# Attention transposes of 64 queries on alternating 64-row tiles, with shared PSUM copies

## The reference, cut to what matters

```python
s_s = jnp.einsum('bcgrd,bcgkd->bcgrk', qs, k_g).astype(jnp.float32) * scale
p_s = masked_softmax(s_s, m_s)
o_s = jnp.einsum('bcgrk,bcgkd->bcgrd', p_s, v_g.astype(jnp.float32))
...
s_w = jnp.einsum('bcgrd,bkgd->bcgrk', qs, kw).astype(jnp.float32) * scale
p_w = masked_softmax(s_w, m_w)
o_w = jnp.einsum('bcgrk,bkgd->bcgrd', p_w, vw.astype(jnp.float32))
...
o = g[..., 0:1] * o_c + g[..., 1:2] * o_s + g[..., 2:3] * o_w
```

## Time and profile before

| | |
|---|---|
| median of three runs | 3684.43 us |
| the profiled execution's own time | 3682.82 us |
| its span, first to last instruction | 3681.0 us |
| PE busy, whole span | 3291.9 us (89%) |
| mean granted TensorE clock | 0.941 of full speed |
| the attention stage, first score to last product | 1963.6 to 2398.6 us |

### The profile page before, as it was taken

How to read it: one execution, slowest core, us unless ns; L and a number is a source line. 1 busy time by engine, 2 the same in 40 slices (tenths; PEclk the granted TensorE clock), 3 DMA queues, 4 the chain that set the end, 5 groups by cost and what they waited for, 6 DMA issues and landing times. The chain is left out here.

```text
span 3681.0 us, 56062 instructions
## 1 busy us (share of the span) xinstructions
PE 3291.9 (89%) x22000; PEld 2951.9 (80%) x22000; DVE 1769.3 (48%) x3212; ACT 942.5 (26%) x1458; POOL 1110.8 (30%) x799
## 2 busy tenths in 40 slices
PE   6886979999999987979667999989687999999986
PEld 5885959999999985869545666657577999999985
DVE  4566046454454446340478888810217454454443
ACT  4544033121111114021124666600114111111111
POOL 1222203333333320323013555400121333333330
PEclk9997979999999997989789999989798999999998
DMA  4213432111111125320231000057202111111112
GB/s 180 73 58 102 145 138 68 46 47 47 46 47 47 46 89 191 119 81 29 99 120 54 2 2 2 2 171 238 98 26 84 47 46 47 47 47 46 47 51 90
DMA packets 75778, 272.75 MB, mean 74 GB/s; under 512 B 9306, under 2 KB 19938, under 8 KB 73330
## 3 DMA queue, kind: packets, MB, share of 16 engines
q1 hardware_dynamic: 73810, 262.99, 20.6%
q10 hardware_dynamic: 1728, 6.34, 0.4%
HBM read 245.47 MB, written 33.10 MB: 76 GB/s over the span
## 5 line engine op out<-in xcount | busy, mean ns | idle before, releaser
L1407 POOL TENSOR_TENSOR w_hi<-w_raw,misc 128x1024 fp32r<-128x1024 f32 x197 | 381.0, 1934 | 2050.5 <-DMA w_raw<-in_w 783.6
L1409 POOL TENSOR_TENSOR w_lo<-w_raw,w_hi 128x1024 fp32r<-128x1024 f32 x197 | 495.1, 2513 | 28.4 <-issue 0.4
L1612 PE MATMUL PA<-hB_hi,w_hi 128*128 128x344 f32 x1512 | 327.9, 326 | 47.4 <-DVE hB_lo L613 23.2
L1612 PE MATMUL PB<-hB_hi,w_hi 128*128 128x344 f32 x1488 | 319.1, 323 | 19.8 <-DVE hB_lo L1796 17.1
L1612 PE MATMUL PB<-hB_lo,w_hi 128*128 128x344 f32 x1488 | 317.6, 322 | 19.5 <-POOL w_lo L1409 19.5
L1612 PE MATMUL PA<-hB_lo,w_hi 128*128 128x344 f32 x1512 | 324.6, 323 | 0.0
L1612 PE MATMUL PA<-hB_hi,w_lo 128*128 128x344 f32 x1416 | 301.9, 322 | 0.0
L385 DVE SCALAR_TENSOR_TENSOR zb<-ub,vec,zb 128x1024 f32<-128x1024 f32 x48 | 158.3, 3297 | 297.1 <-ACT zb L357 297.1
L1612 PEld LDWEIGHTS PA<-hB_hi,w_hi 128*128 128x128 f32 x1512 | 257.2, 191 | 53.2 <-issue 23.9
L1612 PE MATMUL PB<-hB_hi,w_lo 128*128 128x344 f32 x1392 | 294.7, 320 | 0.0
L1612 PEld LDWEIGHTS PB<-hB_hi,w_hi 128*128 128x128 f32 x1488 | 251.9, 189 | 22.9 <-issue 18.3
(11 more groups left out here) (438 smaller groups left out, 6275.6 us busy)
## 6 DMA issues: line engine op xcount, KB each, us to landing
w_raw<-in_w SPq DMA_DIRECT2D x197, 512.0 KB, 3.3
pages<-in_pages SPq DMA_DIRECT2D x64, 384.0 KB, 4.2
cosT<-in_mw SPq DMA_DIRECT2D x32, 512.0 KB, 3.8
sinT<-in_mw SPq DMA_DIRECT2D x32, 512.0 KB, 4.5
mt<-in_mw SPq DMA_DIRECT2D x32, 512.0 KB, 3.9
x_dram<-X SPq DMA_DIRECT2D x3, 4128.0 KB, 12.0
X<-x_dram SPq DMA_DIRECT2D x3, 4128.0 KB, 13.7
mw<-in_mw SPq DMA_DIRECT2D x4, 2048.0 KB, 22.8
```

The lines of the kernel that those rows point to most:

```text
L1407: pool.tensor_tensor(w_hi[b], w_raw[b], zero.broadcast_to([P, 1024]), ALU.add)
L1409: pool.tensor_tensor(w_lo[b], w_raw[b], w_hi[b].bitcast(F32), ALU.subtract).then_inc(sem("w_split"), 1)
L1612: mm = pe.matmul(PS[ps][:, c, 0:CH], w[:, w0:w0 + P], x[:, k, c * CH:(c + 1) * CH], start=(k == 0 and n == 0), stop=(k == K - 1 and n == 2))
```

## The change

Each 128 x 128 transpose becomes two of 64 queries: rows 0 to 63 of the `ring` tile (e = 0) go to bank PC, rows 64 to 127 (e = 1) to bank PD, one after the other, so that neighbours use the array's two 64-row tiles. A bank now holds 64 queries of both halves, not 128 of one half. All transposes of a group wait for both halves' probabilities and for all copies of the group before, and both `t*_done` come with the last pair. `pt` is two buffers of [128, 2, 512] instead of four of [128, 512]; a copy writes runs of 64 at a distance of 128. ACT copies PC in every group and PD in odd groups; DVE copies PD in even groups only. `pt_even_ready` and `pt_odd_ready` take the place of `pt1_ready`.

```diff
@@ transposes(g) on TensorE
+            pe.wait_ge(sem("p_ready"), 2 * (2 * j + tiles[-1][0]) + 2)
+            after(pe, sem("pt0_ready"), g)
+            after(pe, sem("pt_even_ready"), (g + 1) // 2)
+            after(pe, sem("pt_odd_ready"), g // 2)
             for half in range(2):
-                pe.wait_ge(sem("p_ready"), 2 * (2 * j + tiles[-1][0]) + half + 1)
-                after(pe, sem(f"pt{half}_ready"), g)
                 for n, (b, k, x) in enumerate(tiles):
-                    mm = pe.transpose(PCD[half][:, n * P:(n + 1) * P], ring[half][:, x * P:(x + 1) * P], ident)
-                mm.then_inc(sem(f"t{half}_done"), 1)
+                    for e in range(2):
+                        q = slice(64 * e, 64 * e + 64)
+                        c = half * 256 + n * 64
+                        mm = pe.transpose(PCD[e][:, c:c + 64], ring[half][q, x * P:(x + 1) * P], ident[q, q])
+                        if half == 1 and n == len(tiles) - 1:
+                            mm.then_inc(sem(f"t{e}_done"), 1)
@@ values(g) on TensorE
-            pe.wait_ge(sem("pt1_ready"), g + 1)
+            pe.wait_ge(sem("pt_odd_ready" if g % 2 else "pt_even_ready"), g // 2 + 1)
-                                   pt[2 * (g % 2) + half][:, n * P:(n + 1) * P], start=(b == 0 and k == 0),
+                                   pt[g % 2][:, half, n * P:(n + 1) * P], start=(b == 0 and k == 0),
@@ copies
+    def half_rows(g, e):
+        n = len(GROUPS[g][1])
+        to = pt[g % 2][:, :, 0:n * P].rearrange("p h (n q) -> p h n q", q=P)[:, :, :, 64 * e:64 * e + 64]
+        return to, PCD[e].rearrange("p (h n q) -> p h n q", h=2, q=64)[:, :, 0:n, :]
@@ copy_out(g) on ACT
-            act.activation(pt[2 * (g % 2)][:, 0:n], PCD[0][:, 0:n], ACT.Copy).then_inc(sem("pt0_ready"), 1)
+            to, of = half_rows(g, 0)
+            act.activation(to, of, ACT.Copy).then_inc(sem("pt0_ready"), 1)
+            if g % 2:
+                act.wait_ge(sem("t1_done"), g + 1)
+                to, of = half_rows(g, 1)
+                act.activation(to, of, ACT.Copy).then_inc(sem("pt_odd_ready"), 1)
@@ maxima(g) on DVE
-                after(dve, sem(f"t{half}_done"), EVICTED[g])
+                if half == 0:
+                    after(dve, sem("t0_done"), EVICTED[g])
+                    after(dve, sem("t1_done"), EVICTED[g])
@@ copy_out(g) on DVE, now called for even g alone
-            dve.tensor_copy(pt[2 * (g % 2) + 1][:, 0:n], PCD[1][:, 0:n]).then_inc(sem("pt1_ready"), 1)
+            to, of = half_rows(g, 1)
+            dve.tensor_copy(to, of).then_inc(sem("pt_even_ready"), 1)
```

More of the change, by code:

```diff
@@ L183, in build @@
     wmask = awbuf("wmask", [P, 640])
-    pt = [awbuf(f"pt{i}", [P, 512]) for i in range(4)]
+    pt = [awbuf(f"pt{i}", [P, 2, 512]) for i in range(2)]
     mt2 = [kvbuf(f"mt2_{i}", [P, NPR], F32, 33024 + 4096 * i) for i in range(2)]
@@ L933, in att_pe @@
                 values(s - LAG - 1)
+    def half_rows(g, e):
+        n = len(GROUPS[g][1])
+        to = pt[g % 2][:, :, 0:n * P].rearrange("p h (n q) -> p h n q", q=P)[:, :, :, 64 * e:64 * e + 64]
+        return to, PCD[e].rearrange("p (h n q) -> p h n q", h=2, q=64)[:, :, 0:n, :]
     def att_act(act):
         def copy_out(g):
-            n = len(GROUPS[g][1]) * P
             act.wait_ge(sem("t0_done"), g + 1)
             after(act, sem("pv_done"), g - 1)
-            act.activation(pt[2 * (g % 2)][:, 0:n], PCD[0][:, 0:n], ACT.Copy).then_inc(sem("pt0_ready"), 1)
+            to, of = half_rows(g, 0)
[4 more added lines that the diff above has]
+                act.activation(to, of, ACT.Copy).then_inc(sem("pt_odd_ready"), 1)
         def exps(u):
@@ L997, in att_dve @@
                     dve.reciprocal(psm[:, u % 16, :], psm[:, u % 16, :]).then_inc(sem("sum_inverted"), 1)
-            if 0 <= s - LAG < NG:
+            if 0 <= s - LAG < NG and (s - LAG) % 2 == 0:
                 copy_out(s - LAG)
```

## The result

| | before | after |
|---|---|---|
| median, us (4 runs each) | 3682.47 (3680.46 to 3685.9) | 3642.69 (3638.49 to 3647.9) |
| ratio to before | | 0.9892, 95% interval 0.9875 to 0.9909 |
| profiled execution, us | 3682.8 | 3638.5 |
| its span, us | 3681.0 | 3636.6 |
| attention stage, us | 435.1 | 394.9 |

The account below looks back on a forecast made before the run. TensorE's sequence T, S, V was taken to bound the attention stage; -22.8 + 1 + 3 + 1 = -17.8 us took the profiled 3682.8 to 3665.0, and 1.6 for the median gave 3666.5 us, range 3655 to 3686 (0.84).

Parts of the forecast that it names:

- What bounds the kernel: Attention stage before: TensorE's sequence T, S, V sets the time, its matmuls busy for 426.7 of 435.1 us.
- rival C: Transposes: a load waits for its own tile's matmul, a pair takes 0.163 us; 3714 us; chance 0.09 with harsher forms.
- Step 1: Transposes: T is bound by its loads, 8 pairs x 0.108 = 0.86 us for four tiles.
- Step 2: T to S: same tile shape removes the gap, S follows 0.155 us sooner, 147 times: -22.8 us; no other T cost.
- Step 3: Even groups' copies: all of the next T waits for DVE's copy, 6.7 us against 5.6 now: +1 us.
- a sign that step 3 or 4 is wrong: TensorE's idle time ahead of the PC transposes far above 12 us, or S or V beginning to wait.
- Step 4: Odd groups: ACT's two copies just fit, chain through POOL about even, copies stay 0.60 us: +3 us.
- Step 5: Last five steps, without scores: T and V, some 2.05 us, are shorter than two ACT copies, 2.33: +1 us.
- A: Transposes and joint: a pair of loads takes 2 x 0.062 or the gap stays; 3680 to 3688 us; chance 0.19.
- B: ACT's copies become the bound, 0.60 us becoming 1.05 through writing runs of 64; 3714 us; chance 0.06.

Follow-up runs that it names:

- e6: The changed kernel with ACT copying both banks in every group and DVE copying nothing: 3619.26 us, ratio 0.9827 to before.
- e10: e9 with LAG, the distance in groups between scores and transposes, 6 instead of 5: 3615.79 us, ratio 0.9817 to before.
- e1: The changed kernel with all transposes of queries 0 to 63 first, then all of 64 to 127: 3655.47 us, ratio 0.9928 to before.
- e2: The changed kernel with its transposes issued as ordinary f32 products with the identity, two passes each: 3773.93 us (one run).
- e11: The changed kernel with TensorE's last two waits ahead of T swapped, the wait for DVE's copy last: 3641.76 us, ratio 0.9884 to before.
- e9: e6, but DVE copies PD in one group of nineteen, eight in all: 3620.60 us, ratio 0.9829 to before.

## Why the prediction was wrong, step by step

**What bounds the kernel.** Right: TensorE's sequence set the time before, and what T lost came off. It sets it less now, which e6 and e10 show. (Two slips without weight: 3665.0 and 1.6 are 3666.6, and rival C counts 109 groups of four where 108 have an S behind T.)

**Step 1, the transposes: the step that failed.** It says that a pair of loads takes 0.108 us because the scores alternate between two 64-row tiles as the new transposes do. The likeness was the wrong one: tile shape and alternation were the same, but the operation was not. I had the right number in hand, 0.062 us for transposes of 48 rows, and treated it as a far bound, doubled for the two tiles, although had shown two tiles side by side. What two tiles do side by side was in the earlier trace rows, what a transpose's load takes in the earlier trace rows; I should have joined these two. With 0.0625 in the place of 0.108 the same working gives 8 x 0.0455 = 0.36 us more for four tiles, 0.27, 0.18 and 0.09 for three, two and one; over 108, 8, 24 and 7 groups 46.5 us, and with the 22.8 a gain of 69.3. Measured were 71.6. The range did not hold the time because its lower end came from a spread around a wrong term, without this case in it.

**Step 2, the joint.** Right. S's first load is 0.06 behind the last pair, the normal distance, where it stood 0.20 behind the last transpose's start. Transposes and products of one tile shape follow each other without a gap.

**Step 3, copies of even groups.** The mechanism was right, the whole of T does wait for DVE's copy, but the size was off: 6.7 us forecast, 31.5 measured, so that what I had written in step 2, that the new T has no cost besides, its extra waits being met long before, is wrong in 48 places. A large part follows from step 1. I had taken T's place to be 0.155 us earlier per step; it is 0.53 earlier, and DVE, which stays the same, is overtaken in 48 places rather than 17. How the waits hang on T's length is seen in e1 and e2: with T at 0.80 us, near the 0.86 of the forecast, about 15 us in 34 places stand behind DVE's copies, and with 1.78 none but at the end. By this 6.7 would have been too low by half even with a T as long as I had it, and the rest follows from step 1. Another part, in after as in e1, is the wait of 0.10 us that stands behind (e11), some 5 us of the 31.5 by 48 x 0.10, of which 2.8 came back in the stage. Besides, S began to wait for the maxima (3.4 us between T and S), which I had named as a sign that step 3 or 4 is wrong. So the gain in T was spent in part where the faster engine ran into its neighbour.

**Step 4, ACT's second copies and POOL's chain.** +3 us forecast, less than 1 measured in after, where DVE's even copies hold TensorE back first. In e6, with DVE out of the way, 2.8 us in 7 places stand behind POOL, and ACT's copies hold T up for some 11 more. The shape costs nothing, as I had taken it; lines of ACT's and DVE's copies in after:

```profile
L956 ACT ACTIVATE pt<-PD x76: 272/592/597, 1975.3 to 2354.0; 128x512 f32<-128x512 f32 x56, 128x256 f32<-128x256 f32 x12, 128x384 f32<-128x384 f32 x4, 128x128 f32<-128x128 f32 x4
...
L1002 DVE COPY pt<-PD x76: 291/690/693, 1973.5 to 2352.6; 128x512 f32<-128x512 f32 x56, 128x256 f32<-128x256 f32 x12, 128x128 f32<-128x128 f32 x4, 128x384 f32<-128x384 f32 x4
```

0.592 and 0.690 us with runs of 64, against 0.597 and 0.690 in the earlier trace rows.

**Step 5, the end.** Small either way: T to V in the last steps fell from 4.5 to 3.0 us, and work behind the stage took the same time, 1281.7 against 1282.4 us.

**The rivals.** A needed a pair to take 2 x 0.062 or the gap to stay; both are refuted by the pairs at 2169.72 and the load at 2170.21. B's premise is refuted by the copy's 0.592 us, and e6 shows that ACT carries twice as many. C needed a load to wait for its own tile's matmul; the pairs come 0.06 apart while each matmul's record is 0.22 long. None of the rivals was on the side where the result fell: I had listed three ways to gain less and none to gain more.

**What stays open.** Whether the 0.062 us of a transpose is set by its load of 128 columns or by its matmul was not tried; the two follow each other too closely in the records. The 2.8 us of S to V (up to 0.03 in the usual step) have no cause that I tested.

## What to carry to other kernels

Take the rhythm of an operation from rows of the same operation, not of the same shape: a transpose's weight loads follow each other here in little more than half the time of an f32 product's, and two 64-row tiles run side by side at the price of one, so splitting eight transposes into alternating halves took them from 0.87 to 0.49 us. When the engine that bounds a stage gets faster, price anew the waits for its neighbours with its new places; here a copy was better off on the engine that was the busier of the two in total (e6: ACT 322 us, DVE 276); giving eight single places back to the other gained nothing (e9). Where several waits stand ahead of one instruction, put the one that ends last at the end: 0.10 us at each late place here, too little in all to show in the time.

## What the hardware showed that I had not expected

- A weight load for a transpose (f32, 128 columns) comes every 0.061 to 0.0625 us, for a product pass every 0.107 to 0.111 us, on the same tile with the same source (after and e2).
- TensorE begins work of the other tile ahead of the program's order: PD's first load began with three of PC's still to come, and S's first on PA came 0.13 us before PD's last (e1).
- A wait that stands behind the last to be met cost 0.10 us (0.22 against 0.12, e11); more than one behind it was not tried.
- With a change of the array's tile shape from transpose to product a gap of some 0.09 us stood ahead of the product's load (1.02 us from T to S in the earlier trace rows, of which 0.93 are loads and streaming); within one shape there is none (the load at 2170.21 comes 0.06 behind the last pair, as the pairs do among themselves).
